# Attention's division moved behind the weighted sums, and the output turned back

## The reference

```python
s = jnp.einsum('bqhd,bkwhd->bhqkw', qr, kb).astype(jnp.float32) + bias
s = jnp.where(col_ok[:, None, :], s, -jnp.inf)
pr = jax.nn.softmax(s.reshape(bsz, B_HEADS, GRID_W, kh * GRID_W), axis=-1)
pr = pr.reshape(s.shape).astype(vb.dtype)
return jnp.einsum('bhqkw,bkwhd->bqhd', pr, vb)
```

## Time and profile before

| | |
|---|---|
| median of 3 runs | 3674.84 us (3670.18 to 3675.35) |
| the profiled execution | 3673.93 us, of which the span is 3672.1 |
| TensorE (PE) busy | 3507.9 us, 96% of the span |
| VectorE (DVE) busy | 1806.4 us, 49% |
| ScalarE (ACT) busy | 956.9 us, 26% |
| mean granted TensorE clock | 0.984 of 2.4 GHz |

### The profile page before, as it was taken

How to read it: one execution, slowest core, us unless ns; L and a number is a source line. 1 busy time by engine, 2 the same in 40 slices (tenths; PEclk the granted TensorE clock), 3 DMA queues, 4 the chain that set the end, 5 groups by cost and what they waited for, 6 DMA issues and landing times.

```text
span 3672.1 us, 60660 instructions
## 1 busy us (share of the span) xinstructions
PE 3507.9 (96%) x26620; PEld 3322.1 (90%) x26620; DVE 1806.4 (49%) x3040; ACT 956.9 (26%) x1511; POOL 85.7 (2%) x86
## 2 busy tenths in 40 slices
PE   7999999999996899999999999999999869999997
PEld 6999999888875899999999999998888649999997
DVE  5443445644677443333453534466366664333334
ACT  3221223112344321211331212232132523211212
POOL 0000000000001000000000100000000010000000
PEclk9999999999998999999999999999999989999998
DMA  3122123230041212222122222132200512122121
GB/s 132 60 75 80 49 69 102 70 118 19 11 152 61 92 57 70 61 63 70 58 75 68 82 69 64 59 105 83 103 3 20 202 40 64 59 68 66 54 71 57
DMA packets 75943, 264.30 MB, mean 72 GB/s; under 512 B 8402, under 2 KB 8402, under 8 KB 73504
## 3 DMA queue, kind: packets, MB, share of 16 engines
q1 hardware_dynamic: 72128, 248.08, 20.4%
q0 software_dynamic: 3552, 12.34, 1.1%
HBM read 230.50 MB, written 29.88 MB: 71 GB/s over the span
## 4 chain that ended last, share of the span: by engine, by line
PE 90%; DVE 6%; issue 1%; ACT 1%; POOL 0%; DMA 0%; DVEq 0%; SPq 0%; POOLq 0%
PE ps L739 90%; DVE uv L2172 1%; PE ps L1219 0%; DVE rstd L1721 0%; DVE sc L2226 0%; DMA x<-xT 0%; DVE hl L1729 0%; DVE NR L1957 0%; POOL sums L729 0%; DVE yab L2180 0%; ACT mh L1650 0%; ACT L1440 0%; DVE xab L2166 0%; DVE xab L2167 0%; PE ps L1139 0%
## 5 line engine op out<-in xcount | busy, mean ns | idle before, releaser
L739 PE MATMUL ps<-hh,wh 128*128 128x384 f32 (+2 forms) x3520 | 1186.9, 337 | 24.5 <-DVE wl L1711 23.4
L739 PE MATMUL ps<-hl,wh 128*128 128x384 f32 (+2 forms) x3520 | 1178.7, 335 | 0.0
L739 PE MATMUL ps<-hh,wl 128*128 128x384 f32 (+2 forms) x3520 | 1178.1, 335 | 0.0
L739 PEld LDWEIGHTS ps<-hh,wh 128*128 128x128 f32 x3520 | 662.8, 188 | 47.0 <-issue 29.5
L739 PEld LDWEIGHTS ps<-hl,wh 128*128 128x128 f32 x3520 | 662.8, 188 | 15.1
L739 PEld LDWEIGHTS ps<-hh,wl 128*128 128x128 f32 x3520 | 662.7, 188 | 14.2
L1356 ACT CAST wh<-wring 128x1024 fp32r<-128x1024 f32 (+2 forms) x372 | 345.9, 954 | 675.1 <-PE ps L739 657.2
L739 PE MATMUL ps<-act_high,wl 128*128 128x384 f32 x1408 | 470.3, 334 | 0.0
L739 PE MATMUL ps<-act_high,wh 128*128 128x384 f32 x1408 | 470.3, 334 | 0.0
L739 PE MATMUL ps<-act_low,wh 128*128 128x384 f32 x1408 | 470.3, 334 | 0.0
L1835 DVE TENSOR_TENSOR silu<-ps,rstd 128x384 f32<-128x384 f32 x176 | 98.0, 557 | 698.8 <-PE ps L739 698.8
(11 more groups left out here) (264 smaller groups left out, 3517.8 us busy)
## 6 DMA issues: line engine op xcount, KB each, us to landing
wring<-wa SPq DMA_DIRECT2D x244, 512.0 KB, 3.6
wring<-wa SPq DMA_DIRECT2D x64, 384.0 KB, 3.2
wring<-wa SPq DMA_DIRECT2D x64, 320.0 KB, 3.0
bias<-bias SPq DMA_DIRECT2D x24, 512.0 KB, 6.8
conv_q_k<-stage SPq DMA_DIRECT2D x28, 384.0 KB, 2.6
kern_rows<-kst POOLq DMA_DIRECT2D x12, 512.0 KB, 4.0
outT<-x SPq DMA_DIRECT2D x2, 3072.0 KB, 10.2
kern<-kern_rows SPq DMA_DIRECT2D x2, 3072.0 KB, 12.4
```

The source lines that it names most:

```text
L739: return pe.matmul(out, lhsT, rhs, start=start, stop=stop)
```

## The change

The scaling of the exponentials is taken out of `normed`, which keeps the reciprocal. `turn` waits for the exponentials. `weigh` swaps its operands: `pT` is stationary (128 queries), the values move (64 columns), and the result has queries on partitions, in the lower half of bank 6. A new step on VectorE, `scaled`, multiplies the 128x256 result by the reciprocals into `wsc`. A new step on TensorE, `back`, transposes `wsc` in two 128x128 blocks into the upper half of bank 6, and ScalarE's copy waits for that, one iteration later and ahead of `exps`. The loops of TensorE and ScalarE have 16 iterations.

```diff
+        wsc = aft("wsc", [P, 2, 2, HD])
                 def turn(k):
                     n = QUADS * l + k
-                    pe.wait_ge(s_pn, n + 1)
+                    pe.wait_ge(s_pr, n + 1)
...
                     for e in range(2):
-                        for kt in range(2):
-                            j = 2 * e + kt
-                            for a in range(2):
-                                m = mm(ps[64 * a:64 * a + 64, 6, 256 * (n % 2) + P * e:256 * (n % 2) + P * e + P], v_of(l, 2 * hp_ + a, g0 + e, kt),
-                                       pT[:, n % 2, a, P * j:P * j + P], kt == 0, kt == 1)
+                        for a in range(2):
+                            c0 = P * e + HD * a
+                            for kt in range(2):
+                                j = 2 * e + kt
+                                m = mm(ps[:, 6, c0:c0 + HD], pT[:, n % 2, a, P * j:P * j + P], v_of(l, 2 * hp_ + a, g0 + e, kt),
+                                       kt == 0, kt == 1)
                     m.then_inc(s_pv, 1)
 
-                for k in range(QUADS + 3):
+                def back(k):
+                    n = QUADS * l + k
+                    pe.wait_ge(s_ws, n + 1)
+                    for e in range(2):
+                        m = pe.transpose(ps[:, 6, 256 + P * e:256 + P * e + P],
+                                         wsc[:, e, :, :].rearrange("p a h -> p (a h)"), cs("ident"))
+                    m.then_inc(s_bk, 1)
+
+                for k in range(QUADS + 4):
                     if k < QUADS:
                         scores(k)
+                    if k >= 4:
+                        back(k - 4)
...
-                    if k >= 3:
+                    if 3 <= k < QUADS + 3:
                         weigh(k - 3)
...
-                    sa.wait_ge(s_pv, n + 1)
-                    got = ps[:, 6, 256 * (n % 2):256 * (n % 2) + 256]
+                    sa.wait_ge(s_bk, n + 1)
+                    got = ps[:, 6, 256:512]
...
+                    if k >= 4:
+                        weighed(k - 4)
                     if k < QUADS:
                         exps(k)
                     if 2 <= k < QUADS + 2:
                         turned(k - 2)
-                    if k >= 3:
-                        weighed(k - 3)
...
+                    if n >= SCB:
+                        ve.wait_ge(s_ws, n - SCB + 1)
                     step(ve.reciprocal(rsum[:, b, :], ssum[:, b, :]))
-                    for u in range(4):
-                        m = TS(sc[:, b, u, :], sc[:, b, u, :], rsum[:, b, u:u + 1], None, M)
-                    m.then_inc(s_pn, 1)
+
+                def scaled(k):
+                    n = QUADS * l + k
+                    ve.wait_ge(s_pv, n + 1)
+                    if n:
+                        ve.wait_ge(s_bk, n)
+                    by = rsum[:, n % SCB, :].rearrange("p (a e) -> p e a", a=2).unsqueeze(3).broadcast_to([P, 2, 2, HD])
+                    TT(wsc[:, :, :, :], ps[:, 6, 0:256].rearrange("p (e a h) -> p e a h", e=2, a=2), by, M).then_inc(s_ws, 1)
...
                     if 2 * k < len(TAIL_ITEMS):
                         tail_item(l, 2 * k + 1)
+                    if k >= 3:
+                        scaled(k - 3)
```

More of the change, by code:

```diff
@@ L304, in build @@
         s_ql, s_vd, s_cl = sem("q_k_loaded"), sem("v_decode_loaded"), sem("conv_loaded")
-        s_sc, s_sm, s_pr, s_pn = sem("scores_ready"), sem("scores_biased"), sem("exp_done"), sem("probs_normed")
+        s_sc, s_sm, s_pr = sem("scores_ready"), sem("scores_biased"), sem("exp_done")
+        s_ws, s_bk = sem("attn_out_scaled"), sem("attn_out_turned")
         s_tr, s_tc, s_pv, s_pvc = sem("probs_turned"), [sem(f"turned_copied{a}") for a in range(2)], sem("attn_out"), sem("attn_out_copied")
@@ L1254, in attention @@
                         tail_item(l, 2 * k + 1)
-                    if k >= QUADS:
+                    if QUADS <= k < QUADS + 3:
                         for t in (2 * (k - QUADS), 2 * (k - QUADS) + 1):
```

## The result

The changed kernel takes 3697.46 us (median of 6 runs, 3693.24 to 3699.15) against 3674.55 of before beside it: 1.0063 of it, 95% interval 1.0051 to 1.0075. It is slower by about 23 us; the forecast was 3698. The profiled execution has a span of 3696.1 us, 24.0 above that of before.

The account below looks back on a forecast made before the run. TensorE, busy in 96% of the span, was taken to bound the kernel; per layer 0 + 5.2 + 2.0 + 0.1 - 0.9 + 5.3 = +11.7 us, +23.4 for two, giving 3698 us, range 3684 to 3710.

Parts of the forecast that it names:

- the walk: Attention, layer 0: TensorE's time from one score product to the next, summed by stretches to +11.7 us; layer 1 repeats it.
- Part 1: Weighed sum on TensorE: loading 128 stationary columns sets the pace, 16 passes of 0.112 us plus 0.15, +0.92 us a quad.
- The row with one moving column: Profile before: 128 stationary columns and a single moving one take 1.49 us for 12, 0.113 each, so the load sets the pace.
- Rival A: Weighed sum: moving columns set the pace, it stays near 1.08 us; +1.4 us a layer, 3677; chance 0.08.
- Part 2: Turn back on TensorE: two transposes a quad and a gap cost 0.32 us, between 0.22 and 0.5.
- Part 4(b): Turn back in iterations 4 to 7 waits for VectorE's scaling behind the odd tail item: 0.1 to 0.15 us of stall.
- Part 4(c): Weighed sum waits for ScalarE's copy of the previous quad: 0.35 us in iteration 8, 0.6 and 1.55 in the tail.
- rival C: Tail of attention: new stalls bring TensorE's half clock in both layers, +3 to +5 us a layer, 3705; chance 0.18.
- Rival B: Attention: VectorE bounds the stage, so its saved 0.7 us a quad takes 16.8 us off, 3657; chance 0.04.

Follow-up runs that it names:

- the run with 32 columns: Changed kernel with each product of the weighed sum split in two of 32 moving columns, 32 passes a quad instead of 16: 3771.87 us, one run.
- the kernel with the late squares: Changed kernel with ScalarE's two squares of iterations 12 and 13 moved to 14 and 15, behind the copies of the turned-back results: 3689.97 us, one run.

## Why the prediction was right

Its time is within a microsecond, and that closeness is luck: the two main terms are in the right place with the right cause, but two misses of opposite sign, -1.4 us in iterations 4 to 7 and +2.8 in the tail of layer 0, meet in the sum, and layer 1 grew by 1.5 less than walked. For layer 0, by the walk:

| stretch | walked | measured |
|---|---|---|
| iterations 0 to 3 | 0 | -0.2 |
| 4 to 7 | +5.2 | +3.8 |
| 8 and 9 | +2.0 | +1.8 |
| 10 | +0.1 | +0.1 |
| 11, to the turn of 12 | -0.9 | -1.2 |
| tail | +5.3 | +8.1 |
| stage | +11.7 | +12.5 |

**Part 1 was right in kind and 0.04 to 0.21 too high.** The row with one moving column decided for the load, and the passes of the new shape take (1.90 - 0.26)/15 = 0.109 us. I took 0.112 and a gap of 0.15 everywhere; the slot is 1.73 to 1.90, and in iterations 4 to 7 the swap adds 0.80, 0.71, 0.70 and 0.79, not 0.92. The run with the operands put back shows that it is the swap that costs (14.8 us), and the run with 32 columns shows that the load is what costs in it. Rival A has fallen: the moving columns did not set the pace.

**Part 2 was 0.05 too high** (0.27 instead of 0.32; 0.36 in iteration 4).

**Part 4(b), the wait of the turn back for VectorE, didn't come** in iterations 4 to 7 of the changed kernel: the turn back starts right behind the scores. It did come in iteration 12, 0.52 us. The estimate for the item's own VectorE part was right, 0.47 for the 0.46 that I took; too long were the 0.27 of drain and wake-up and the item's 0.85. In iteration 6 the item fills 0.79, VectorE starts 0.11 us after the end of its slot at 1099.16, and the scaling ends at 1100.16, just ahead of TensorE at 1100.23 (timeline of VectorE):

```profile
1099.27 0.55 DVE L2158 TENSOR_TENSOR olocal<-olocal,ps 128x384 f32<-128x384 f32 x1 [1.27 <-PE ps L741]
1099.74 0.42 DVE L2258 TENSOR_TENSOR wsc<-ps,rsum 128x256 f32<-128x256 f32 x1
```

Parts 1, 2 and 4(b) are the 1.4 us by which iterations 4 to 7 were overpriced: 0.7, 0.1 and 0.6. Three smaller errors beside them cancel. The turns and items filled 0.6 us less than before. The wait for the copy behind a logarithm, which I had walked in iteration 8 alone (0.35), came in iterations 7 and 8 (0.44 and 0.43). And the 0.33 that I took off in iteration 7 was no idle of TensorE (the slots of the scores were 0.2 shorter over the four all the same): the row "issue" is the way from TensorE to VectorE, where the chain leaves TensorE for the smoothing, the exponentials and a logarithm up to 1103.45, so that it isn't TensorE piece after piece from iteration 4 to 9 either. The timeline of PE before, start of iteration 7:

```profile
1096.93 1.13 PE L739 MATMUL ps<-kT,qT 64*128 64x256 f32 x8
1098.02 0.89 PE L739 MATMUL ps<-tmp,cst 128*128 128x384 f32 x2
```

**Part 4(c), the copy's wait in the tail, was the right place with the right cause and too small a price.** I walked 0.6 and 1.55 and it was 0.96 and 1.83. ScalarE began 0.2 after the conv turns' slot ended and its copy ended 2.0 after it, where I had 1.87, and TensorE began another 0.2 after the copy; the walk had neither of these wake-ups. The larger part is what it set off. I gave the half clock 0.18 as rival C, and it came, in both layers: 1.6 on the weighed sum, 0.7 on the conv turns and 0.3 on the last turn back of layer 0. C's own price, 3 to 5 a layer, was too high for that stretch of 2.6. The forecast without C was too low for the tail, and the stretches before made 2.0 of its 2.8 good. The evidence that I weighed against C, idles of 0.70 to 1.90 in iterations 10 to 12 of layer 0 without a fall, says little: in layer 1 of the same execution the same 1.90 was followed by one, and with the old operands 1.83 was too. What decides whether the clock falls behind such an idle, these runs don't tell: behind 0.96 it fell in layer 1 of the changed kernel, and behind 1.10 it held in the kernel with the late squares.

**Rival B, the other side, was worth 4.2 us** in the run without the division, not 17, and it came in iterations 3 and 11, two of the places that the prediction had named; iteration 10 gave nothing. Adding up: 14.8 for the swap, 9.1 for the copy's wait and its clock, and nothing for the rest, 23.9 against 22.9 measured (3697.46 - 3674.55).

Layer 1's stage grew by 10.2 us, 2.3 less than layer 0's: 1.2 because its tail before had a half-clock stretch already, and 1.2 in iterations 0 to 3, which ran at 0.76 of the clock before and 0.91 after. The two stages give 22.7 of the span's 24.0. Of the rest, Hyena of layer 0 was 0.8 shorter and the stretch from the output projection's first product to that of the feed-forward's second matrix was 1.6 longer (173.4 us against 171.8), with half clock in it after and none beyond its first 3 us before. Which of the shifts in the clock belong to the change and which to chance, the two profiled executions can't tell.

## What to carry to other kernels

A product with a small moving side pays for its stationary side: before swapping the operands of a matrix product, count the stationary columns loaded and whether two such products could share the array, not the multiplications. When work goes from one engine to another, take the gain from the stretches where the first one is waited for and the cost from all the others; here that was 4 us against 15. And a buffer that is handed on through one more engine lengthens every wait on it: look where the work that covered it runs out, here at the end of the loop and in the two iterations with a logarithm, and what stands ahead of the release in that engine's own order.

## What the runs showed that I had not expected

TensorE's clock fell with the engine busy. With 32 moving columns a pass it was busy 89.4 of 93.0 us in the window above and granted 0.81, with several stretches at 1.2 GHz; the first in the window shows in the reads of 1090.80, when TensorE had been busy without a gap since 1076.4. With 64 columns a pass and at most 0.16 of idle ahead of the weighed sums of the tail it was granted 1.00 throughout, and with 64 columns and idles of 0.96 and 1.83 us it fell to 1.2 GHz, behind the longer one in layer 0 and already behind the shorter one in layer 1. The same idles with the old operands brought a stretch at 1.2 GHz as well: that tail's window has a mean of 0.89.

```profile
1130.80 1.97 PE L741 MATMUL ps<-pT,vwin 128*64 128x128 f32 x16 [1.83 <-issue]
...
1120.00:1135.20 15.20, 11.26 (x96) 9.50 (x97) 4.94 (x10) 7.27 (x17) 0.00 (x0) 0.89 0.44 169
```

The Trainium skill's remark on the page "TensorE: Matmul & The Clock Gate", section "Part 4: PE-mode transpose", that transposes don't count as activity for the clock, isn't settled by these runs: two transposes a quad more left it at 1.00 in every iteration from 4 to 12 of layer 0, between other products.

The other thing is the edge on either side of a change of shape. In iteration 5 the turn ahead of the weighed sum fills 0.87 us where the sum takes the full array and 0.96 where it takes it in halves, and the item behind it 0.80 against 0.84, so that the swap's 0.70 us there costs 0.57 in the iteration. No trace here tells what makes these edges.
